# Two SwiGLU layers with seven-product panels: which DMA makes which weight sum, and in what order ScalarE and VectorE take the pieces

## What is computed

```python
def swiglu(h, w_gu, w_down):
    u = h @ w_gu
    g, v = u[..., :D_FF], u[..., D_FF:]
    return (jax.nn.silu(g) * v) @ w_down
...
        h = h + swiglu(rmsnorm(h, norm_g[layer, 1]), ffn_w_gu[layer], ffn_w_down[layer])
```

## Time and profile before

| | us |
|---|---|
| median of 3 runs | 2192.06 (2189.43 to 2197.82) |
| the profiled execution | 2194.57 |
| its span, first to last instruction | 2192.7 |
| TensorE busy in the span | 2089.8 (95%) |
| VectorE busy | 1399.3 (64%) |
| ScalarE busy | 968.6 (44%) |
| GpSimd busy | 443.4 (20%) |

### The profile page before, as it was taken

One profiled execution on the slowest core, in us unless ns is written; L12 is line 12 of the kernel. 1 busy time (PEld: TensorE's weight loads), 2 busy tenths in 40 slices (PEclk: granted clock), 3 DMA queues, 4 the chain that ended last, 5 costly groups with the idle time before them and its releaser, 6 DMA issues.

```text
span 2192.7 us, 32213 instructions
## 1 busy us (share of the span) xinstructions
PE 2089.8 (95%) x11914; PEld 1636.4 (75%) x11914; DVE 1399.3 (64%) x2072; ACT 968.6 (44%) x1602; POOL 443.4 (20%) x426
## 2 busy tenths in 40 slices
PE   8999999999999999999989999999999998999998
PEld 6787888889878877888788888877778885333336
DVE  7887966766687678875766666678875455000038
ACT  6556634334343444774643434355452233212143
POOL 1334521212110054000521211120000013222220
PEclk9999999999999999999999999999999999999999
DMA  5321477777623352122477777622122148999961
GB/s 206 114 105 58 137 184 178 186 188 181 170 84 135 135 166 79 31 44 87 126 187 188 179 178 177 163 99 77 58 98 105 68 163 325 412 414 411 382 252 58
DMA packets 97193, 361.20 MB, mean 165 GB/s; under 512 B 17920, under 2 KB 18304, under 8 KB 69142
## 3 DMA queue, kind: packets, MB, share of 16 engines
q1 hardware_dynamic: 54080, 282.58, 35.2%
q0 software_dynamic: 42592, 76.50, 16.4%
q10 hardware_dynamic: 416, 0.70, 0.1%
HBM read 347.34 MB, written 22.48 MB: 169 GB/s over the span
## 4 chain that ended last, share of the span: by engine, by line
PE 54%; DMA 19%; DVE 11%; issue 8%; ACT 5%; POOL 3%; SPq 1%; DVEq 0%; ACTq 0%; POOLq 0%
PE psum L735 13%; PE psum L736 13%; PE psum L737 12%; DMA w_sum<-a_raw 6%; DMA w_sum<-w_a 4%; PE psum L1550 4%; DMA panel<-w_m 4%; PE psum L1574 3%; DMA a_raw<-w_sum 2%; PE psum L1239 2%; PE psum L1214 1%; DVE h L2508 1%; DVE a_lo L2409 1%; POOL w_sum L3593 1%; POOL a_raw L3592 1%
## 5 line engine op out<-in xcount | busy, mean ns | idle before, releaser
L735 PE MATMUL psum<-hn_hi,a_hi 128*128 128x512 f32 (+2 forms) x952 | 379.1, 398 | 1.9 <-DVE a_lo L2398 0.9
L737 PE MATMUL psum<-hn_hi,a_lo 128*128 128x512 f32 (+2 forms) x952 | 369.5, 388 | 0.0
L736 PE MATMUL psum<-hn_lo,a_hi 128*128 128x512 f32 (+2 forms) x952 | 369.2, 388 | 0.0
L735 PE MATMUL psum<-tx_hi,slot_hi 128*128 128x256 f32 x640 | 187.7, 293 | 44.5 <-ACT pc L1899 44.3
L735 PEld LDWEIGHTS psum<-hn_hi,a_hi 128*128 128x128 f32 (+1 forms) x952 | 176.8, 186 | 48.9 <-issue 8.2
L736 PEld LDWEIGHTS psum<-hn_lo,a_hi 128*128 128x128 f32 (+1 forms) x952 | 177.0, 186 | 39.9 <-issue 2.7
L737 PEld LDWEIGHTS psum<-hn_hi,a_lo 128*128 128x128 f32 (+1 forms) x952 | 176.8, 186 | 39.3
L2409 DVE TENSOR_TENSOR a_lo<-a_raw,a_hi 128x2048 fp32r<-128x2048 f32 (+3 forms) x68 | 155.7, 2290 | 46.8 <-ACT a_hi L1657 46.2
L737 PE MATMUL psum<-tx_hi,slot_lo 128*128 128x256 f32 x640 | 184.3, 288 | 0.0
L736 PE MATMUL psum<-tx_lo,slot_hi 128*128 128x256 f32 x640 | 184.3, 288 | 0.0
L735 PEld LDWEIGHTS psum<-tx_hi,slot_hi 128*128 128x128 f32 x640 | 125.5, 196 | 50.7 <-DVE slot_lo L2692 46.6
(11 more groups left out here) (578 smaller groups left out, 4668.7 us busy)
## 6 DMA issues: line engine op xcount, KB each, us to landing
a_raw<-w_a SPq DMA_DIRECT2D x115, 1024.0 KB, 5.4
panel<-w_m SPq DMA_DIRECT2D x96, 1024.0 KB
b_raw<-w_b SPq DMA_DIRECT2D x64, 512.0 KB, 3.5
w_sum<-w_a SPq DMA_DIRECT2D x80, 256.0 KB, 7.3
w_sum<-a_raw POOLq DMA_DIRECT2D x80, 256.0 KB
a_raw<-a_raw POOLq DMA_DIRECT2D x40, 256.0 KB
a_raw<-w_sum POOLq DMA_DIRECT2D x40, 256.0 KB
q_scratch<-q_hi POOLq DMA_DIRECT2D x7, 384.0 KB
```

The costliest lines, as they stand in the source:

```text
L735: pe.matmul(out, w_hi, x_hi, start=first, stop=False, skip_group_check=again)
L736: pe.matmul(out, w_hi, x_lo, start=False, stop=False, skip_group_check=again)
L737: return pe.matmul(out, w_lo, x_hi, start=False, stop=last, skip_group_check=again)
```

## The change

Line numbers below are those of the kernel before. Three things change in both stages.

**Loads.** `w_sum[v]` is filled by one DMA of 512 KB with A_21 and A_22, in place of two of 256 KB with A_11 and A_21. It now stands ahead of the load of the raw panel, and waits until all DMAs of the panel two before have landed, S_4 included, and its S_1 has been split. The load of the raw panel waits for the split of S_4 as well as of A_22.

**Sums.** `sum_panel` falls in two. `sum_early` adds A_11, read from memory, to `w_sum` S_3, waits for it to land, and adds S_3 to S_2; it needs no raw panel. `sum_late` makes S_1 and then S_4 in the raw panel. GpSimd runs the early part of each panel ahead of the late part of the panel before it. The number of added DMAs (four for each panel) is the same.

**Order.** S_2 is rounded before S_3. In A, `copy_2` now stands ahead of `high_1` and `high_s4` on ScalarE, and the hidden tile ahead of them on both engines; in B, S_2 of the next panel moves ahead of `high_a22`. TensorE's order stays.

The diff, cut to its core:

```diff
-            def load_fast(a, b, q):
+            def load_fast_pair(a, b, g, i):
+                for v in range(2):
+                    if i > 1:
+                        sp.wait_ge(w_summed[v], summed_at(g) + 64 * i - 64)
+                        sp.wait_ge(w_split, split_at(g) + 10 * i + 5 * v - 15)
+                    sp.dma_start(w_sum[:, v, :, :, :].rearrange("p a k n -> p (a k n)"),
+                                 w_a[ds(a + v + 2 * i, 1), :, 2 * S:4 * S].rearrange("a p n -> p (a n)")) \
+                      .then_inc(sum_begun[v], 16)
+                    if i > 1:
+                        sp.wait_ge(w_split, split_at(g) + 5 * (2 * i + v - 3) + 2)
+                    load_a(a + v, i)
+                    load_b(b + v, i)
+
+            def load_fast(a, b, q, g):
                 sp.wait_ge(hn_ready, KT * (q + 1))
-                with sp.Fori(1, FF_TILES // 2) as i:
-                    for v in range(2):
-                        load_a(a + v, i)
-                        for x, c in ((S_2, 0), (S_3, 2 * S)):
-                            sp.dma_start(w_sum[:, v, x, :, :].rearrange("p k n -> p (k n)"),
-                                         w_a[ds(a + v + 2 * i, 1), :, c:c + S].rearrange("a p n -> p (a n)")) \
-                              .then_inc(sum_begun[v], 16)
-                        load_b(b + v, i)
+                for i in range(1, FF_TILES // 2):
+                    load_fast_pair(a, b, g, i)
+                sp.wait_ge(w_split, split_at(g + 1) - 4)
...
+                pe.wait_ge(w_split, split + 3)
                 seven(x, P_6, *tx(T2), again=True).then_inc(w_used, 2 if first else 1)
                 if not first:
                     pe.wait_ge(a_ready, n)
                     pe.wait_ge(part_added, added_at(g) + 2 * m)
                     seven(bank[3 - 2 * v][:, 0:HALF], P_4, *tx(T4), again=True).then_inc(tile_ready, 2)
                 pe.wait_ge(part_added, added_at(g) + 2 * m + 1)
+                pe.wait_ge(w_split, split + 4)
                 seven(z, P_7, *tx(T3)).then_inc(w_used, 1)
                 pe.wait_ge(part_copied, copied + 2)
                 pe.wait_ge(w_split, split + 5)
...
             def high_s3(sa, g, i, v):
                 m = v - 2 + 2 * i
                 first = isinstance(i, int) and m == 0
+                act.wait_ge(w_summed[v], summed_at(g) + 64 * i - 48)
+                if first:
+                    act.wait_ge(tile_ready, 2 * sa + 2)
+                else:
+                    act.wait_ge(w_used, used_at(g) + 6 * (m - 1) + 5)
+                act.activation(slot_hi[:, P_7, :, :], w_sum[:, v, S_3, :, :], ACT.Copy).then_inc(w_rounded, 1)
+
+            def high_s2(sa, g, i, v):
+                m = v - 2 + 2 * i
+                first = isinstance(i, int) and m == 0
                 act.wait_ge(w_summed[v], summed_at(g) + 64 * i - 32)
                 if first:
                     act.wait_ge(tile_ready, 2 * sa + 2)
                 else:
-                    act.wait_ge(w_used, used_at(g) + 6 * (m - 1) + 5)
-                act.activation(slot_hi[:, P_7, :, :], w_sum[:, v, S_3, :, :], ACT.Copy).then_inc(w_rounded, 2 if first else 1)
-
-            def high_s2(sa, g, i, v):
+                    act.wait_ge(w_used, used_at(g) + 6 * (m - 1) + 4)
+                act.activation(slot_hi[:, P_6, :, :], w_sum[:, v, S_2, :, :], ACT.Copy).then_inc(w_rounded, 2 if first else 1)
+
...
             def fast_a(sa, sb_, e, i, g):
                 copy_1(g, i, 0)
+                high_b(sb_ - 1, i)
+                silu(e, i - 1, 1)
+                copy_2(sa, g, i, 0)
+                high_a22(sa, i, 0)
+                high_hid(1, hid_made, hid_at(g) - 2 + 2 * i)
                 high_1(sa, g, i, 1)
                 high_s4(g, i, 0)
-                silu(e, i - 1, 1)
-                copy_2(sa, g, i, 0)
-                high_b(sb_ - 1, i)
-                high_a22(sa, i, 0)
-                high_hid(1, hid_made, hid_at(g) - 2 + 2 * i)
                 copy_3(g, i, 0)
+                high_s2(sa, g, i, 1)
                 high_s3(sa, g, i, 1)
-                high_s2(sa, g, i, 1)
                 high_s1(sa, g, i, 1)
                 high_b(sb_, i)
 
@@ -1958,11 +1968,12 @@
                 high_s4(g, i, 1)
                 silu(e, i, 0)
                 copy_2(sa, g, i, 1)
+                if not last:
+                    high_s2(sa, g, i + 1, 0)
                 high_a22(sa, i, 1)
                 high_hid(0, hid_made, hid_at(g) - 1 + 2 * i)
                 if not last:
                     high_s3(sa, g, i + 1, 0)
-                    high_s2(sa, g, i + 1, 0)
                 copy_3(g, i, 1)
                 if not last:
                     high_s1(sa, g, i + 1, 0)
...
@@ -2778,20 +2790,20 @@
                 n, m = sa + 2 * i, 2 * i - 2
                 add_11(g, m, 0)
                 scale_11(g, m, 0)
-                low_1(g, m + 1, 1)
+                low_b(sb_ - 1, i)
                 scale_12(used_at(g) + 6 * m + 3, 1)
-                low_s4(split_at(g) + 5 * m + 7, 0)
                 scale_gate(e, i - 1, 1)
                 add_21(n - 1, 1)
                 fast_hidden(e, n - 1, i - 1, 1)
-                low_b(sb_ - 1, i)
+                low_a22(n, 0)
                 low_hid(e, i - 1, 1)
-                low_a22(n, 0)
+                low_1(g, m + 1, 1)
+                low_s4(split_at(g) + 5 * m + 7, 0)
                 add_22(g, m, 0)
+                low_s2(g, m + 1, 1)
                 low_s3(g, m + 1, 1)
                 for k in range(4):
                     add_y(sb_ - 2 + 2 * i, k)
-                low_s2(g, m + 1, 1)
                 low_s1(g, m + 1, 1)
                 low_b(sb_, i)
                 for k in range(4, KT):
@@ -2808,11 +2820,12 @@
                 scale_gate(e, i, 0)
                 add_21(n, 0)
                 fast_hidden(e, n, i, 0)
+                if not last:
+                    low_s2(g, m + 2, 0)
                 low_a22(n + 1, 1)
                 low_hid(e, i, 0)
                 if not last:
                     low_s3(g, m + 2, 0)
-                    low_s2(g, m + 2, 0)
                 add_22(g, m + 1, 1)
                 if not last:
                     low_s1(g, m + 2, 0)
...
-            def sum_panel(sa, g, i, v):
+            def sum_early(sa, g, i, v):
+                done = summed_at(g) + 64 * i
+                if i > 1:
+                    pool.wait_ge(w_summed[v], done - 64)
+                pool.wait_ge(sum_begun[v], begun_at(g) + 16 * i)
+                pool.dma_start(w_sum[:, v, S_3, :, :].rearrange("p k n -> p (k n)"), w_a[sa + v + 2 * i, :, 0:S],
+                               accum_op=ALU.add).then_inc(w_summed[v], 16)
+                pool.wait_ge(w_summed[v], done - 48)
+                pool.dma_start(w_sum[:, v, S_2, :, :], w_sum[:, v, S_3, :, :], accum_op=ALU.add).then_inc(w_summed[v], 16)
+
+            def sum_late(sa, g, i, v):
                 done = summed_at(g) + 64 * i
                 pool.wait_ge(a_loaded[(sa + v) % 2], 16 * ((sa + v) // 2 + i) + 16)
-                pool.wait_ge(sum_begun[v], begun_at(g) + 32 * i)
+                pool.wait_ge(w_summed[v], done - 32)
                 pool.dma_start(part(v, S_1), part(v, A_22), accum_op=ALU.add).then_inc(w_summed[v], 16)
-                pool.dma_start(w_sum[:, v, S_3, :, :], part(v, A_11), accum_op=ALU.add).then_inc(w_summed[v], 16)
-                pool.wait_ge(w_summed[v], done - 32)
-                pool.dma_start(w_sum[:, v, S_2, :, :], part(v, S_1), accum_op=ALU.add).then_inc(w_summed[v], 16)
                 pool.wait_ge(w_summed[v], done - 16)
                 pool.wait_ge(w_split, split_at(g) + 5 * (v - 2 + 2 * i) + 1)
                 pool.dma_start(part(v, S_4), w_sum[:, v, S_2, :, :], accum_op=ALU.add).then_inc(w_summed[v], 16)
@@ -3600,9 +3620,13 @@
             def ffn(sa, g):
                 for k in range(KT // 2):
                     make_tx(g, k)
+                sum_early(sa, g, 1, 0)
                 for i in range(1, FF_TILES // 2):
-                    for v in range(2):
-                        sum_panel(sa, g, i, v)
+                    sum_early(sa, g, i, 1)
+                    sum_late(sa, g, i, 0)
+                    if i + 1 < FF_TILES // 2:
+                        sum_early(sa, g, i + 1, 0)
+                    sum_late(sa, g, i, 1)
 
             sums(T_FFN0)
             ffn(A_FF0, 0)
```

39 lines of the change are left out of this document (16 added, 23 removed).

## The result

The changed kernel takes 2353.78 us (2348.62 to 2364.06 in 4 runs), the kernel before 2190.94 beside it. The ratio is 1.074, with a 95% interval of 1.070 to 1.079: slower by 163 us. The profiled execution took 2348.62 us with a span of 2346.8, against 2192.7 before, so the two traces are 154.1 us apart. The forecast was 2269, +76 us: right in sign and place, too small by half.

The account below looks back on a forecast made before the run. TensorE, busy 95%, bounds the kernel before; afterwards a ring of sums and fills does. Ring +67, stage starts +15, last pairs -6 give +76 us on 2192.06, rounded to 2269; the ring's bounds give 2220 to 2316, stated range 2165 to 2316.

Parts of the forecast that it names:

- The start of the stages: Chain up to P_6 of the first A in the loop, 44.9 us before copying; +15 us taken for both stages.
- S_3 with its addend from memory: Early sum on GpSimd reading A_11 from memory; taken at 3.5 us, the same as a sum within SBUF.
- The ring: Per panel S_4, next fill, S_3, S_2 with S_1 in series; 39.0 us a pair, bounds 36 and 42, +67 us.
- the last pairs: Last pair of a stage: no further panel is filled, the ring is open and waits go; -6 us.
- part 2: Loop of both stages: the sums become one ring that TensorE must follow, 39.0 us a pair against 34.8.
- part 1: The new orders: A's wait for copy_2 goes; alone worth up to 52.9 us plus the clock, together about 64.
- The raw panel beside S_2 and S_1: Two 1 MB raw panel loads a pair lengthen the ring by 2 us each, between 1 and 3.5.
- The fill with `b_raw`: SyncE's b_raw load shortly ahead of each fill: 5.4 us for both against 3.5, 3.8 us for a pair.
- What is late next: In A after copy_2: low_hid for down, 2.9 us behind P_4, judged covered by TensorE's work.
- the waits go: Rival: the ring is hidden under TensorE and part 1's gain comes in; about 2130 us, chance 0.16 (2115 to 2181).
- Queues take turns: Rival: each load costs the ring under 1.7 us, ring 33.6 to 36.4, upper end 2227 us; chance 0.10.
- The stall costs more than its length: Rival: waits over 5 us in A lower the clock, 1.7 us a pair; 2296 to 2330; over 2316 chance 0.08.

Follow-up runs that it names:

- e1: Changed kernel, but GpSimd issues the four sums of a panel together, then those of the next panel; 2165.45 us, ratio 0.987 to the kernel before.
- e6: Changed kernel, but the addend of S_3 comes from SBUF instead of memory (some sums then wrong); 2280.78 us in one run.
- e4: Kernel before with its own loads and sums, but the new order on ScalarE and VectorE in A; 2172.69 us, ratio 0.989.
- e9: e1, but for the first two panels of a stage S_1 and S_3 are issued together and S_2 behind both; 2155.16 us, ratio 0.984.
- part 3: Experiments on the prices of the ring's steps: three variants of the changed kernel, each shortening one step; 2280.78, 2271.42 and 2278.01 us.
- e10: e1, but ScalarE and VectorE work in A in the old order; 2202.57 us, ratio 1.005 to the kernel before.
- e7: Changed kernel, but each raw panel's load brings only its first half (512 KB); 2271.42 us in one run.
- e11: e3, but with high_b and low_b moved up in A, behind copy_1 and the first additions; 2334.25 us, ratio 1.065.
- e3: Changed kernel with its loads and order of sums, but the old order in A on ScalarE and VectorE; 2406.47 us.

## Why the prediction was right and where it fell short

- **What failed: the size of two terms.** The start of the stages was put at +15 us and was +40, and S_3 with its addend from memory was put at 3.5 us, "the same" as a sum within SBUF, and was 4.6. The time lies 38 us above the upper end of 2316. The ring as a whole was inside its bounds, 41.7 us against 36 to 42, so with an old pair of 34.4 the loop is only 2 us beyond its worst case; the start is 25 us beyond its term, the last pairs 2, and 9 are that the medians lie 163 us apart and the two traces 154.
- **Sign, mechanism and place: right.** The ring of part 2 is there step by step, TensorE waits for L1904 ahead of P_6 of A, ScalarE at L1897, GpSimd at L3606 for the fill. A's wait for `copy_2` is gone, as part 1 said; the 14.4 us left are B's. e1 shows the cause: opening the ring takes the loss away.
- **S_3 with its addend from memory: mis-sized, and without a bound.** The forecast took 3.5 us, "with nothing to say that it is cheaper", and nothing for dearer. It is 4.6 a panel, +2.2 a pair; e6 shows 0.9 of the 1.1 us to be the source. It was named under what would show the forecast wrong, and should have been in the range.
- **The raw panel beside S_2 and S_1: a little low.** 2 us each were taken, within 1 and 3.5; 7.75 less 5.1 is 2.6, +1.3 a pair. The 4.8 and 6.3 us of the earlier trace rows had been cut twice, for size and for "idle latencies".
- **The fill with `b_raw`: a little high.** 5.0 us instead of 5.4, -0.8 a pair (and S_4 as forecast). Together 39.0 has become 41.7: 16 x 2.7 = 43 us of the miss. That 41.7 still lay under 42 is in part luck: the bound was meant for contention, and S_3's addend used most of it. The old pair was 34.4 by the windows above, which both run from P_6 to P_6, and not 34.8, which is 16 x 0.4 = 6 more.
- **The start of a stage: the worst term.** +15 was taken for both, and it was +40. The changed kernel's GpSimd in the first stage, then SyncE:

```profile
267.12 1.11 POOL L3606 DMA_DIRECT2D w_sum<-w_a  x1
271.86 0.89 POOL L3609 DMA_DIRECT2D w_sum<-w_sum  x1 [3.63 <-DMA w_sum<-w_a]
279.51 0.85 POOL L3609 DMA_DIRECT2D w_sum<-w_sum  x1 [5.87 <-DMA w_sum<-w_a]
...
294.07 0.86 POOL L3606 DMA_DIRECT2D w_sum<-w_a  x1 [6.97 <-DMA w_sum<-w_a]
302.14 0.86 POOL L3609 DMA_DIRECT2D w_sum<-w_sum  x1 [7.20 <-DMA w_sum<-w_a]
302.67 1.20 POOL L3615 DMA_DIRECT2D a_raw<-a_raw  x1
307.25 0.86 POOL L3618 DMA_DIRECT2D a_raw<-w_sum  x1 [3.38 <-DMA a_raw<-a_raw]
```

```profile
289.57 0.33 SPq L634 DMA_DIRECT2D w_sum<-w_a  x1
293.63 0.33 SPq L609 DMA_DIRECT2D a_raw<-w_a  x1
294.01 0.42 SPq L617 DMA_DIRECT2D b_raw<-w_b  x1
```

The order of steps is the forecast's. But S_3 at 294.07, priced at 3.5, took 8.07 us, with 1.5 MB of loads issued by SyncE directly before it; the next took 7.85, with a raw load 0.6 us behind it, and the pair at 271.86 took 7.65 instead of 5.1. The chain is 61 us where 44.9 were summed, and only 4 of the difference had been allowed. S_2 with S_1 at 302.14, with nothing beside them, took the priced 5.11. The sum was right where the queues were empty; at the other steps loads that had waited went out together. That these loads are the cause is read from the rows: no run took them away.
- **Last pair:** -6 forecast, -3.6 measured.
- **Part 1 alone** was put at 64 us; e4 gives 23. "What is late next" was sought for `down`'s operands and not for its banks, which wait for VectorE behind the split of S_3. In the changed kernel it made no difference that the traces show, but it is what the rival "the waits go" was priced with: 2130, where e1 and e9 reach 2165 and 2155.
- **Rivals.** "The waits go" is what the same parts give in another issue order, so the sum of the ring was the right thing to decide by. "Queues take turns" had less than 1.7 us for a load; the raw load costs 2.6, and 41.7 is past its ring of 33.6 to 36.4. The Trainium skill, "DMA: Bandwidth & Descriptors", section "Queues, rings and completion order", has each DMA engine go round the queues a packet at a time; this trace does not agree with what was worked out from it for the sums. "The stall costs more than its length" (2296 to 2330) pointed beyond the forecast for a wrong reason, and the time is above it too. The lower clock came behind the wait shown above (window as in rows 2):

```profile
456.38:461.00 4.62, 4.62 (x24) 4.62 (x24) 3.23 (x6) 1.72 (x3) 0.00 (x0) 0.56 0.62 144
```

0.56 is mostly the lower level, 1.2 GHz. But none of the waits of GpSimd counted in part 3 ends with a product, so nothing shows that it lengthened the ring.
- **The range** ended at 2316 because every bound in it was one of contention in the loop. The two terms without a bound, S_3's addend and the start, carry 16 x 2.2 = 35 and 25 us, and with both allowed for the upper end is past 2370.

## What to carry to other kernels

When work is issued ahead on a queue that waits in order, write down for each buffer what frees it and who issues that: if the freeing step stands behind the early work on the same queue, it is a ring, and where it is longer than the work of the other engines, its length and not the bandwidth sets the rate. Compare the issue orders before the loads: here the order of four DMAs was worth 190 us, and what was loaded from where some 10 (e10 against before). See also which load falls beside which step of the ring. Give each price without a row an upper bound, and price the start of a stage with the loads that have queued up for it.

## What the runs showed of the hardware

- An adding DMA of 256 KB whose addend comes from memory (S_3 of e7) lands 4.3 us after its issue on average, one within SBUF (S_3 of e6) 3.4: 0.9 us more for the source.
- The cost of an adding DMA goes with the load beside it: 5.1 us for two with nothing, 5.5 beside 512 KB, 7.75 beside 1 MB; and S_3 took 8.1 behind 1.5 MB. It also goes with when the load is issued: three sums took 12.5 us with the 1 MB load 2.1 us behind the first of them, 11.6 with it 0.8 us behind (e11), and 9.6 with it 4.9 us ahead (e3). The 1 MB load is stretched too, 7.0 us on average in the changed kernel's loop against 5.1 in e1.
- Moving the addend of S_3 from memory to SBUF (e6) also made the sums and the raw load behind it faster, by 1.1 and 1.8 us. No run here says why.
